# Where the buffers start in SBUF: whole 2 KB rows first, on a base rounded to 2 KB

## What is computed

```python
# block 1
h = rms_norm(x, g);  proj = h @ w_in                  # pooling, q, 6 kv slots, gates
x = x + (gate_pool*y_pool + gate_nsa*y_nsa) @ w_out   # attention with compressed,
h = rms_norm(x, g2)                                   # selected and window branches
gate_pre, val = split(h @ w_up, 2)                    # 1024 -> 2 x 2816
x = x + (silu(causal_dwconv(gate_pre)) * val) @ w_down
# twice:
u = rmsnorm(x) @ w_in_2      # short conv, differential attention, 31-tap conv branch
x = x + concat(y_a, y_b, y_c) @ w_out_2
x = x + (silu(h @ w_gate) * (h @ w_up)) @ w_down_2
return rmsnorm(x, final_norm_g)
```

## Time and profile before

| | us |
|---|---|
| median of 3 runs (1936.87 to 1936.93) | 1936.91 |
| the profiled execution | 1937.58 |
| its span, first to last instruction | 1935.8 |
| granted TensorE clock, mean over the span | 0.991 |

### The profile page before, as it was taken

How to read it: one execution, slowest core, us unless ns; L and a number is a source line. 1 busy time by engine, 2 the same in 40 slices (tenths; PEclk the granted TensorE clock), 3 DMA queues, 4 the chain that set the end, 5 groups by cost and what they waited for, 6 DMA issues and landing times.

```text
span 1935.8 us, 29986 instructions
## 1 busy us (share of the span) xinstructions
PE 1892.8 (98%) x8654; PEld 1506.9 (78%) x8654; DVE 854.3 (44%) x1316; ACT 739.0 (38%) x1172; POOL 1109.0 (57%) x1318
## 2 busy tenths in 40 slices
PE   7999999999999999999999999999999999999996
PEld 6876678888888888767888888887767888888885
DVE  7677644455555122766433332121766433323113
ACT  5245553333323223566432332222556433323222
POOL 4442235666667565855556565665864555656564
PEclk9999999999999999999999999999999999999998
DMA  7211112222222323321222222322321222222322
GB/s 247 66 55 44 56 55 98 88 93 101 94 93 96 108 98 99 104 69 58 88 98 98 98 93 99 101 98 100 101 80 61 77 98 98 94 99 89 109 98 87
DMA packets 52036, 178.14 MB, mean 92 GB/s; under 512 B 6512, under 2 KB 7664, under 8 KB 51696
## 3 DMA queue, kind: packets, MB, share of 16 engines
q1 hardware_dynamic: 51952, 177.09, 27.4%
HBM read 169.76 MB, written 2.10 MB: 89 GB/s over the span
## 4 chain that ended last, share of the span: by engine, by line
PE 85%; DVE 4%; issue 2%; POOLq 2%; ACT 2%; POOL 1%; DMA 1%; DVEq 1%; SPq 1%; ACTq 0%
PE bank L535 22%; PE bank L515 21%; PE bank L516 21%; PE bank L572 3%; PE bank L573 3%; PE bank L579 3%; POOLq L476 2%; POOL wl L458 1%; DMA turned<-ybuf 1%; PE bank L772 1%; PE bank L818 1%; PE bank L804 1%; PE bank L555 1%; SPq L428 1%; PE bank L549 1%
## 5 line engine op out<-in xcount | busy, mean ns | idle before, releaser
L458 POOL TENSOR_TENSOR wl<-raw,wh (+1 forms) x1252 | 1027.2, 851 | 754.1 <-ACT wh L1001 754.0
L1001 ACT ACTIVATE wh<-raw 128x1024 fp32r (+1 forms) x313 | 331.8, 1060 | 850.1 <-PE bank L535 708.1
L515 PE MATMUL bank<-xh,wh 128*128 128x512 f32 x1336 | 526.6, 394 | 0.0
L516 PE MATMUL bank<-xl,wh 128*128 128x512 f32 x1336 | 523.6, 392 | 0.0
L535 PE MATMUL bank<-xh,wl 128*128 128x512 f32 x1336 | 341.2, 395 | 0.0
L535 PEld LDWEIGHTS bank<-xh,wl 128*128 128x128 f32 x1336 | 250.6, 189 | 62.0 <-issue 11.1
L515 PEld LDWEIGHTS bank<-xh,wh 128*128 128x128 f32 x1336 | 252.4, 189 | 59.0 <-issue 5.6
L516 PEld LDWEIGHTS bank<-xl,wh 128*128 128x128 f32 x1336 | 252.7, 189 | 52.1
L515 PE MATMUL bank<-hh,wh 128*128 128x512 f32 x528 | 208.0, 394 | 0.0
L516 PE MATMUL bank<-hl,wh 128*128 128x512 f32 x528 | 208.0, 394 | 0.0
L1415 DVE TENSOR_TENSOR ybuf<-bank,rstd 128x512 f32<-128x512 f32 x95 | 65.3, 688 | 239.8 <-PE bank L535 237.7
(11 more groups left out here) (292 smaller groups left out, 2209.4 us busy)
## 6 DMA issues: line engine op xcount, KB each, us to landing
raw<-in_weights SPq DMA_DIRECT2D x313, 512.0 KB, 3.3
turned<-ybuf SPq DMA_DIRECT2D x64, 64.0 KB, 2.0
xs<-in_x SPq DMA_DIRECT2D x4, 512.0 KB, 6.9
out_t<-xs SPq DMA_DIRECT2D x8, 256.0 KB, 2.1
w1k<-in_w SPq DMA_DIRECT2D x1, 1024.0 KB, 9.4
w1v<-in_w SPq DMA_DIRECT2D x1, 1024.0 KB, 10.4
shifted<-kvraw SPq DMA_DIRECT2D x8, 124.0 KB, 2.3
posi<-in_positions SPq DMA_DIRECT2D x2, 256.0 KB, 8.5
```

The costliest lines, as they stand in the source:

```text
L458: x_ = pool.tensor_tensor(wl[:, :, :].rearrange("p s n -> p (s n)")[:, two], raw[:, cols((v % 4) * (CB * P) + h * part, part)], wh[:, :, : ...
L515: mm(b[:, :], w, kh(k), start=first and k == 0, stop=False)
L516: mm(b[:, :], w, kl(k), start=False, stop=False)
L1001: return act.activation(o, i, ACT.Copy, scale=scale)
```

## The change

The buffers are placed in another order, on another base. No instruction is added, removed or moved: on each engine the same operations stand in the same order with the same waits. Only addresses differ.

```diff
-        base = -(-nc.sbuf_base // 64) * 64
+        base = -(-nc.sbuf_base // (4 * S)) * (4 * S)
...
         wl = sb("wl", [P, 2, CB * P], F32R)
-        cst = sb("cst", [P, NC])
-        msk = sb("msk", [P, 2 * P + 256], BF16)
-        pr1 = sb("pr1", [P, NP1])
-        pr2 = sb("pr2", [P, LAYERS * NP2])
-        par = sb("par", [P, NP2])
         cos = sb("cos", [P, S])
...
         sqacc = sb("sqacc", [P, S])
-        small = sb("small", [P, 192])
         ybuf = sb("ybuf", [P, 2, S])
         BIG = top[0]
         UNIT = 4 * S
+        assert BIG % UNIT == 0
...
         tmp = sb("tmp", [P, 2, S])
+        pairs = sb("pairs", [P, S])
         tmp2 = sb("tmp2", [P, 528])
         tmp3 = sb("tmp3", [P, 528])
         small2 = sb("small2", [P, 576])
-        pairs = sb("pairs", [P, S])
+        small = sb("small", [P, 192])
+        cst = sb("cst", [P, NC])
+        msk = sb("msk", [P, 2 * P + 256], BF16)
+        pr1 = sb("pr1", [P, NP1])
+        pr2 = sb("pr2", [P, LAYERS * NP2])
+        par = sb("par", [P, NP2])
```

## The result

The changed kernel takes 1921.75 us (median, 1921.55 to 1923.04), the one before 1936.89 in the same comparison: a ratio of 0.9922, 95% interval 0.9910 to 0.9934. That is 15.1 us faster, where 86 were forecast; the time lies far outside the range of 1830 to 1880 us.

The account below looks back on a forecast made before the run. PE's matmul pace was taken to bound the kernel; gains of 73.9 (dense stretches), 4.8 (input products) and 7 (start) sum to 85.7 us, from 1937.6 to 1851.9, stated as 1851 us, range 1830 to 1880.

Parts of the forecast that it names:

- What bounds the kernel: Whole kernel: PE almost never idle, so time is set by matmul count and starting pace; only the pace can change.
- So the pace goes by the place where the moving row lies: Dense matmuls: moving rows at 128 past a multiple of 256 take 544 cycles, at 64 take 560.
- the law built on it: Moving rows are fetched in 256-byte pieces, the last one's unused tail paid like columns: 32 or 48 cycles.
- Rows 5: Where the weights are the moving rows, at 128: the faster pace, 0.45 us for two matmuls.
- The third case: bf16 mask matmul, 256 columns, ends 32 columns before the boundary; follower 0.12 us later, matching 288 cycles.
- The floor: Aligned 512-column matmuls: the array's own step, about 216 ns, with 213.3 ns as lower bound.
- Rows 7: Plain float32, two cycles a column: 2.16 us for 2560 columns in 8 matmuls, against 2.133 of pure array time.
- Nothing happens: Rival for the whole kernel: pace goes by region or distance, buffers stay in their regions; 1937 us, chance 0.06.
- A start on the boundary costs a whole piece: Rival: fetch always takes nine pieces, so every matmul takes 576 cycles, 240 ns; 2010 us, chance 0.06.
- Something else takes over: Rival in dense stretches: chunk handover or POOL becomes late, half of 74 us lost; 1888 us, chance 0.08.
- The taps on DVE: Vector work does not feel start addresses: taps should stay at 754 ns, and DVE, ACT, POOL cost nothing.
- POOL's period among the taps: Stretches with taps: POOL's 5.82 us per chunk unchanged, limiting the input products' gain to 4.8 of 11.7 us.

Follow-up runs that it names:

- e5: Stand-alone matmul program sweeping the distance between moving and stationary starts, 64 float32r matmuls a series, no kernel computation: 226.7 ns at distance 0, 233.3 at 128.
- e1: Stand-alone program, PE alone running series of 32 matmuls with starts, columns or type varied: float32r 227 to 233 ns, bf16 216 ns.
- e8: Changed kernel with 64 bytes put in ahead of raw, between normalised inputs and weights: 1948.12 us, ratio 1.0056.

## Why the prediction was wrong

**What bounds the kernel** was right: PE's pace and nothing else, with idle PE only where it was named. Each matmul that became quicker in a dense stretch came off the end. The reading of the two paces, 544 and 560 cycles, and of which buffers have which, was right too.

**The step that failed is the sentence "So the pace goes by the place where the moving row lies", and the law built on it.** In the kernel before, the moving `xh`/`xl` stand at 128 modulo 256 and so do the stationary `wh`/`wl`; `hh`, `mh` and `yh` stand at 64. The trace held two values of the moving start and only one of the stationary start, so the start of the moving row and its distance from the stationary block could not be told apart. I took the first. Rows 5, which I cited as another case of 128, has both operands at 128 as well, so it speaks as much for distance 0. The arithmetic that fitted to the cycle (32 columns of tail, 48 columns of tail) was chance: the first is a cost of a float32r matmul that no start address takes away, which e5 shows at distance 0 for 512, 384 and 256 columns, and the second is that cost and 16 for a distance off 256, at 512 columns.

**The third case** that I took as proof, the bf16 mask matmul with 0.12 us to its follower, did not stand for a pace. The bf16 series of e1 take 216 ns at every start. In the mask's row the follower is a float32 matmul; the 0.12 us is there in the kernel after as well. That the tail law doesn't hold for bf16 is shown; where these 0.12 us come from is not.

**The floor** of 216 ns was taken from plain float32. It holds for bf16. No float32r series of 512 columns went below 226.7 ns, and the kernel's faster group had been there all along. In the sum, this is the term that failed: 4968 matmuls were forecast to gain 10.7 ns each and gained nothing (53 us of 94), and 2352 were to gain 17.3 and gained 6.7 (25 us). These 78 us are just 7320 times the 10.7 ns between 216 and 226.7. Rows 7 show eight records of four matmuls: each plain float32 matmul of the program leaves two, so the two cycles a column read there are those of one record.

**The rivals.** None was right as written. "Nothing happens" had the half that matters: it asked whether the pace goes by "region or distance", and then weighed both as one, for a change that "leaves every buffer in its region". It did not leave the distances: `BIG` came closer to `wh` by 5,568 bytes. The address table ahead of the prediction has the numbers. "A start on the boundary costs a whole piece" fell with the law. (Its sum has 3312 and 2205 matmuls in the dense stretches; 4968 - 600 - 1092 = 3276 and 2241 are right, which moves it by less than 1 us. The 3312 stands in the expectation of e8 too.) "Something else takes over" has no sign in the trace: POOL is busy 300 of 460 us in the dense stretch.

**Smaller steps.** The taps on DVE and the rest of the vector work don't feel the addresses: the row of line 1373 after has the same figures as the earlier trace rows:

```profile
L1373 DVE SCALAR_TENSOR_TENSOR bank<-cpad,par,bank x60: 754/755/757, 771.0 to 1378.4; 128x512 f32<-128x512 f32 x60
```

POOL's period among the taps has stayed, 5.85 us against 5.82, as forecast; the input products' matmuls are of the group that gained nothing, so there was next to nothing to lose there. Timeline of POOL after:

```profile
782.90 2.84 POOL L459 TENSOR_TENSOR wl<-raw,wh 128x256 fp32r<-128x256 f32 x4
...
788.75 2.84 POOL L459 TENSOR_TENSOR wl<-raw,wh 128x256 fp32r<-128x256 f32 x4
```

The chances were wrong in kind. A law read off two points and one odd case got 0.80 of them, and the range was made from the uncertainty of the sum under that law. Such a law also had a simple weaker form, "the slow group comes down to the fast one", which needed no step beyond any row of the trace: 2352 x 6.7 = 15.7 us, 1921 us. It should have stood among the cases.

## What to carry to other kernels

Put the moving and the stationary operands of float32r matmuls with 512 columns a multiple of 256 bytes apart (at 256 columns the series shows no gain from it); 64 bytes of padding did here what a new layout did. When one instruction has two paces in a trace, tabulate every operand's address and the differences between them before fitting a law to one of them, and don't extrapolate to an address that no row shows: the gain that rows bear out is that of the slow group reaching the fast one.

## What the runs showed of the hardware

- A float32r matmul of 128 x 128 by 512 columns starts every 544 cycles (226.7 ns) at the full clock when its operands start a multiple of 256 bytes apart, and every 560 (233.3 ns) at most other distances; 550 at 64 modulo 256 (in the kernel 233.3 ns were seen there too), 565 at 4. The absolute start is without effect (0, 32, 64, 128 were tried in the kernel).
- Its 32 cycles over the column count are the same for 512, 384 and 256 columns (544, 416, 288), but 128 columns take 264 cycles. They don't go away with fewer stationary columns. The 16 cycles for distance 128 at 512 columns are 6 at 384, and none at 256. bf16 has 216 ns for 512 columns, at any start tried (0 to 192). Plain float32 leaves two records for a matmul of the program, 429 to 430 ns apart for 512 columns at distance 0 and at 64, about two cycles a column in each.
- That the load of the next stationary block and the stream of the moving rows disturb each other in SBUF would fit all of this, since they run side by side. That is argued and not shown: the profile has no counter for it, and narrower stationary blocks give no clear answer. At distance 0 they made the stream slower (552 cycles with 64 columns, 556 with 32), at distance 128 quicker (554 with 32, against 560).
